# A projection's piece between two links of the inversion: one row of blocks instead of two

## The reference

```python
proj = einsum('bsd,dc->bsc', rmsnorm(x, ln_mix_pre), w_in)
qkv = silu(conv5(proj[q, k, v]))            # depthwise, 5 taps
qa, ka = l2norm(q) * 128**-0.5, l2norm(k)
o_a = delta(qa, ka, va, g_f, beta_f) + flip(delta(flip(qa), flip(ka), flip(va), ...))
o_a = rmsnorm(o_a, norm_a) * silu(z)
# delta, for each chunk: solve (A + I) [u, w] = [v*beta, k*beta*exp(gc)],
# A strictly lower triangular, then a scan over the chunks:
#   v_new = u - w @ state;  o = (q*exp(g)) @ state + a_qk @ v_new
#   state = state * exp(g_last) + (k*exp(g_last - g)).T @ v_new
```

## Time and profile before

| | us |
|---|---|
| median of three executions | 3401.22 |
| lowest, highest | 3398.41, 3410.64 |
| the profiled execution | 3407.34 |
| its span, first to last instruction | 3405.5 |
| TensorE busy in the span | 3172.8 |
| VectorE, ScalarE, GpSimd busy | 1510.9, 1055.3, 366.0 |
| mean granted clock of TensorE | 0.964 |

### The profile page before, as it was taken

One profiled execution on the slowest core, in us unless ns is written; L12 is line 12 of the kernel. 1 busy time (PEld: TensorE's weight loads), 2 busy tenths in 40 slices (PEclk: granted clock), 3 DMA queues, 4 the chain that ended last, 5 costly groups with the idle time before them and its releaser, 6 DMA issues.

```text
span 3405.5 us, 38831 instructions
## 1 busy us (share of the span) xinstructions
PE 3172.8 (93%) x16207; PEld 2581.3 (76%) x16207; DVE 1510.9 (44%) x2112; ACT 1055.3 (31%) x2290; POOL 366.0 (11%) x433
## 2 busy tenths in 40 slices
PE   7999999988899998989989999999999999998997
PEld 4788878877787877877844688888888876777876
DVE  4465555666653122121113344444444567532452
ACT  3444343444433222222310133112112234213452
POOL 0122232232221000000000000000000011001111
PEclk9999999999999998988989999999999999997998
DMA  2211111111011101111261412111111220111010
GB/s 103 63 52 48 37 48 49 34 29 33 29 41 59 59 35 47 38 40 42 91 233 43 170 52 70 50 50 50 50 50 50 93 90 25 62 38 44 26 38 25
DMA packets 59313, 194.86 MB, mean 57 GB/s; under 512 B 7649, under 2 KB 15329, under 8 KB 49410
## 3 DMA queue, kind: packets, MB, share of 16 engines
q1 hardware_dynamic: 58272, 191.29, 16.4%
q10 hardware_dynamic: 866, 1.09, 0.1%
HBM read 158.37 MB, written 33.98 MB: 56 GB/s over the span
## 4 chain that ended last, share of the span: by engine, by line
PE 80%; DVE 9%; ACT 7%; issue 2%; DMA 1%; POOL 1%; SPq 0%; ACTq 0%; POOLq 0%; DVEq 0%
PE ps L2288 18%; PE ps L2290 17%; PE ps L2289 17%; PE ps L1987 5%; PE ps L2165 3%; PE ps L706 3%; PE ps L700 3%; PE ps L1663 2%; DVE ar L1096 2%; PE ps L3166 2%; PE ps L712 1%; PE ps L1628 1%; PE ps L743 1%; PE ps L737 1%; PE ps L3123 1%
## 5 line engine op out<-in xcount | busy, mean ns | idle before, releaser
L2288 PE MATMUL ps<-r,r 128*128 128x512 f32 (+2 forms) x2656 | 1056.8, 398 | 34.3 <-DVE r L228 6.1
L2290 PE MATMUL ps<-r,r 128*128 128x512 f32 (+2 forms) x2656 | 1006.1, 379 | 0.0
L2289 PE MATMUL ps<-r,r 128*128 128x512 f32 (+2 forms) x2656 | 1005.1, 378 | 0.0
L2288 PEld LDWEIGHTS ps<-r,r 128*128 128x128 f32 x2656 | 515.8, 194 | 128.9 <-issue 19.1
L2290 PEld LDWEIGHTS ps<-r,r 128*128 128x128 f32 x2656 | 512.8, 193 | 95.5
L2289 PEld LDWEIGHTS ps<-r,r 128*128 128x128 f32 x2656 | 515.6, 194 | 82.0 <-issue 5.1
L2288 PE MATMUL ps<-r 128*128 128x512 f32 x512 | 199.7, 390 | 0.8 <-DVE r L2281 0.8
L2290 PE MATMUL ps<-r 128*128 128x512 f32 x512 | 199.2, 389 | 0.0
L2289 PE MATMUL ps<-r 128*128 128x512 f32 x512 | 199.2, 389 | 0.0
L2538 DVE TENSOR_TENSOR ar<-ar,ps 128x512 f32<-128x512 f32 x224 | 150.9, 685 | 92.2 <-PE ps L2290 92.1
L1987 PE MATMUL ps<-ar 128*128 128x512 f32 x384 | 170.9, 604 | 8.6 <-DMA ar<-sc_o 6.6
(11 more groups left out here) (319 smaller groups left out, 4287.9 us busy)
## 6 DMA issues: line engine op xcount, KB each, us to landing
ar<-wst SPq DMA_DIRECT2D x76, 1024.0 KB, 4.9
ar<-wst SPq DMA_DIRECT2D x52, 512.0 KB, 3.6
ar<-x SPq DMA_DIRECT2D x16, 512.0 KB, 9.3
ar<-sc_g SPq DMA_DIRECT2D x32, 256.0 KB, 4.7
sc_h<-ar SPq DMA_DIRECT2D x32, 256.0 KB, 2.1
sc_x<-ar SPq DMA_DIRECT2D x16, 512.0 KB, 2.7
ar<-sc_x SPq DMA_DIRECT2D x16, 512.0 KB, 4.3
sc_b<-ar SPq DMA_DIRECT2D x24, 260.0 KB, 2.0
```

The costliest lines, as they stand in the source:

```text
L2288: t.do.matmul(o, l[0], r[0], start=first, stop=False)
L2289: t.do.matmul(o, l[0], r[1], start=False, stop=False)
L2290: return t.do.matmul(o, l[1], r[0], start=False, stop=last)
```

## The change

A piece of a projection becomes one row (three products) with a yield behind it, so the prep and fill threads have twice the slots in every order. The other engines keep their steps: `halved` puts each into the first of two slots and leaves the second empty. The flips keep their rows (13 and 15), the turned tiles of x in the opening order follow the rows 0, 2, 4 and 6. The counts and shapes of the instructions are the same.

```diff
-        plan = [merged((("prep", 0), 2 * NPREP, 0.0, 1.0), (("gates",), 14, 0.15, 0.75), (("bias",), 13, 0.3, 1.0))]
+        plan = [merged((("prep", 0), 4 * NPREP, 0.0, 1.0), (("gates",), 14, 0.15, 0.75), (("bias",), 13, 0.3, 1.0))]
...
-                threads.append((("prep%d" % part, h + 1), NPREP + 8 * (h + 1 in GATES), 0.0, 1.0))
+                threads.append((("prep%d" % part, h + 1), 2 * NPREP + 16 * (h + 1 in GATES), 0.0, 1.0))
...
-                threads.append((("fill", 8 + part), 16, 0.0, 1.0))
+                threads.append((("fill", 8 + part), 32, 0.0, 1.0))
...
-                    if kt % 2 == 1:
-                        yield
+                    yield
...
-                if h == 0 and n < 4:
-                    pe_turn_x(t, 4 + n)
+                if h == 0 and n < 8 and n % 2 == 0:
+                    pe_turn_x(t, 4 + n // 2)
...
-                if n in (6, 7):
-                    pe_flip(t, h, "fq", n - 6, chq[h % 2])
+                if n in (13, 15):
+                    pe_flip(t, h, "fq", (n - 13) // 2, chq[h % 2])
...
+        def halved(steps):
+            for _ in steps:
+                yield
+                yield
...
-                    return both(act_prep0(a, 0), act_prep1(a, 0))
+                    return halved(both(act_prep0(a, 0), act_prep1(a, 0)))
```

More of the change, by code:

```diff
@@ L661, in pe_prep1 @@
                 for n, _ in enumerate(pe_proj(t, h, s)):
-                    if n in (6, 7):
-                        pe_flip(t, h, f, n - 6, src)
+                    if n in (13, 15):
+                        pe_flip(t, h, f, (n - 13) // 2, src)
                     yield
@@ L1036, in make @@
                 if what == "prep":
-                    return both(act_prep0(a, 0), act_prep1(a, 0))
-                return {"gates": act_gates, "prep0": act_prep0, "prep1": act_prep1, "inv": act_inv, "scan": act_scan, "fin": act_fin, "bias": act_bias, "qk": act_qk, "fill": act_fill, "split": act_first_split}[what](a, *of)
+                    return halved(both(act_prep0(a, 0), act_prep1(a, 0)))
+                return {"gates": act_gates, "prep0": lambda a, h: halved(act_prep0(a, h)), "prep1": lambda a, h: halved(act_prep1(a, h)), "inv": act_inv, "scan": act_scan, "fin": act_fin, "bias": act_bias, "qk": act_qk, "fill": lambda a, h: halved(act_fill(a, h)), "split": act_first_split}[what](a, *of)
             for order in plan:
@@ L1248, in make @@
                 if what == "prep":
-                    return both(dve_prep0(v, 0), dve_prep1(v, 0))
+                    return halved(both(dve_prep0(v, 0), dve_prep1(v, 0)))
                 if what == "bias":
                     return idle(1)
-                return {"qk": dve_qk0, "fill": dve_fill, "gates": dve_gates, "prep0": dve_prep0, "prep1": dve_prep1, "inv": dve_inv, "scan": dve_scan, "fin": dve_fin, "split": dve_first_split}[what](v, *of)
+                return {"qk": dve_qk0, "fill": lambda v, h: halved(dve_fill(v, h)), "gates": dve_gates, "prep0": lambda v, h: halved(dve_prep0(v, h)), "prep1": lambda v, h: halved(dve_prep1(v, h)), "inv": dve_inv, "scan": dve_scan, "fin": dve_fin, "split": dve_first_split}[what](v, *of)
             for order in plan:
@@ L1325, in make @@
                 if what == "prep":
-                    return both(idle(NPREP), pool_prep1(p, 0))
-                return idle(1) if what in ("gates", "prep0", "bias", "qk", "fill", "split") else {"prep1": pool_prep1, "inv": pool_inv, "scan": pool_scan, "fin": pool_fin}[what](p, *of)
+                    return halved(both(idle(NPREP), pool_prep1(p, 0)))
+                return idle(1) if what in ("gates", "prep0", "bias", "qk", "fill", "split") else {"prep1": lambda p, h: halved(pool_prep1(p, h)), "inv": pool_inv, "scan": pool_scan, "fin": pool_fin}[what](p, *of)
             for order in plan:
@@ L1404, in make @@
                 if what == "prep":
-                    return both(sp_prep0(sp, 0), sp_prep1(sp, 0))
-                return idle(1) if what in ("scan", "split") else {"gates": sp_gates, "prep0": sp_prep0, "prep1": sp_prep1, "inv": sp_inv, "fin": sp_fin, "bias": sp_bias, "qk": sp_qk, "fill": sp_fill}[what](sp, *of)
+                    return halved(both(sp_prep0(sp, 0), sp_prep1(sp, 0)))
+                return idle(1) if what in ("scan", "split") else {"gates": sp_gates, "prep0": lambda sp, h: halved(sp_prep0(sp, h)), "prep1": lambda sp, h: halved(sp_prep1(sp, h)), "inv": sp_inv, "fin": sp_fin, "bias": sp_bias, "qk": sp_qk, "fill": lambda sp, h: halved(sp_fill(sp, h))}[what](sp, *of)
             for order in plan:
```

## The result

The changed kernel takes 3482.9 us (3480.5 to 3488.9) against 3401.4: the ratio is 1.023, with a 95% interval of 1.021 to 1.025. I had forecast 3443 with 3405 to 3464. It is slower, as forecast, but by 81.5 us where the sum said 42. The profiled execution took 3485.0 (span 3483.1), 2.1 above the median, and its span is 77.6 us longer than the one of before.

The account below looks back on a forecast made before the run. TensorE was taken to bound the kernel, 875.8 us busy of a 957 us stage. Losses of 64.3 less gains of 22.0 gave 42 us slower, from 3401 to a median of 3443, range 3405 to 3464.

Parts of the forecast that it names:

- What bounds it: Recurrent heads stage, 957 us: TensorE bounds it, busy 875.8 us, so a reordering can win or lose only its idle time.
- the mechanism: Engines work queues in order, so a link's copy waits behind a step that waits for a later row; losses 64.3 us.
- Term (a): All eight gate parts: squares or scaled copies stand ahead of Y6's copy on ScalarE; 1.2 us each, 9.6 in all.
- (b): Eight gate parts: an eviction stands ahead of Y5's copy, making it 0.65 us late; 5.2 in all.
- (c): Eight gate parts: an eviction of the gates stands ahead of T1's copy, 0.65 us late; 5.2 in all.
- (d): Ends of odd parts: state update queued behind z's gating product, next part's first state product 4.2 us late; 9.8 in all.
- (e): Parts 1 to 7: convolution step (odd parts also small norm products) ahead of X4's masked copy on VectorE; 8.6 us.
- (f): Plain parts (8 to 15): evictions, flipped keys' copy and squares, and convolution steps ahead of links' copies; 23.8 us in all.
- Rival 3: Ends of odd parts: each 4.2 us stall may bring a clock fall, 12 to 17 us more, 3458; chance 0.17.
- Rival 2: Inside parts: losses are absorbed by shorter waits at the starts of parts; 15 us slower, 3416; chance 0.14.
- Rival 1: Whole stage: evenly spread cover wins and evictions find their row done; 24 us gained, 3377; chance 0.09.
- The gains: TensorE's waits at links, the first Y and the opening, covered by the finer order: 19.3, 2.0 and 0.7, 22.0 us.

Follow-up runs that it names:

- run with GpSimd behind: Changed kernel, but in the four odd parts with a gate GpSimd's two additions start only behind VectorE's last small product of the norms; 3471.2 us, ratio 1.019.
- all steps late: Changed kernel's one-row pieces, but the steps of ScalarE, VectorE, GpSimd and SyncE put by `later` into the second of their two slots; 3382.7 us, ratio 0.9928.

## Why the prediction was wrong in size

The forecast's terms, summed by part, against the differences of the two traces (start of one part to the start of the next):

| parts | forecast | measured |
|---|---|---|
| 0, 2, 4, 6 | +13.0 | +14.2 |
| 8, 10, 12, 14 | +3.5 | +4.6 |
| 1, 3, 5, 7 | +22.3 | +38.1 |
| 9, 11, 13 | +5.0 | +22.4 |
| opening, part 15 and all behind | -1.4 | -1.7 |

- **What bounds it and the mechanism** were right. Each engine worked its queue in order and a link's copy stood behind a step that waited for a later row. The same instructions with the other engines' steps one slot apart differ by 100 us.
- **Term (a)**, 1.2 us: T6 leaves 1.1 to 1.4 us late in all eight parts; taken back alone it is 11.5 us for 9.6.
- **(b), (c)**: from start to start T5 and X1 leave 0.65 to 0.7 us late in parts 0, 2, 4 and 6, as forecast. In the odd ones T5 is 0.4 to 0.7 late, and X1 only 0.3 in parts 3 and 7. The even parts, which have hardly other terms, come out within 1.2 us of the forecast over four parts. They were not taken back singly.
- **(d)**, the size of the wait: 4.2 late was forecast, the rows show 4.1 seven times, and the w waits behind it went at all seven, the ones of L743 at four. Only the clock behind it was left out of the sum.
- **(e)** was mis-sized. It was priced at 1.4 in odd parts with a gate and Y5 was 2.9 to 3.1 us late (in parts 2, 4 and 6 it was 0.5 for the 1.0 forecast). I had taken the small products at what they take alone, though the trace of before already holds four of 1.25 us beside GpSimd's addition:

```profile
474.05 1.25 DVE L1143 TENSOR_TENSOR ar<-ar 128x8 f32<-128x8 f32 x1
```

  The run with GpSimd behind shows their 2 us, and 11.7 us of the time in all; without them the longest wait of Y is 1.1. The Trainium skill, "SBUF — State Buffer" (Who interferes with whom), states this very rule: a VectorE instruction with both inputs in SBUF contends with a GpSimd instruction that reads SBUF, and the one that comes second waits until the other is done. The trace agrees (1.23 and 1.12 us against 0.15). The sum left it out, since the change touches no instruction of either engine. But in the kernel before these products stood behind X4's masked copy (471.32 in the earlier trace rows, the product at 474.05), where Y5 did not wait for them, and the change put them ahead of it.
- **(f)** missed two places in parts 9, 11 and 13: from start to start Y2 waits 1.28 us where it waited 0.19, and Y5 1.16 where it waited 0.58. That is 5 us. So my list of slots was incomplete, and it also lacked the row that is gone ahead of the first Y in these parts (above, 3.1 us). T2, forecast 2.6 late, was:

```profile
752.39 0.60 PE L641 MATMUL ps<-ar 128*128 128x128 f32 x4
...
754.83 0.58 ACT L989 ACTIVATE ar<-ps 128x512 f32<-128x512 f32 x1
755.46 1.40 PE L705 MATMUL ps<-ar 128*128 128x128 f32 x8 [2.47 <-ACT ar L989]
```

- **Rival 3, the clock**, was no alternative to the sum but a part of it, and that is the step that failed: the sum put the clock at nothing, and TensorE is busy 29.7 of the 79.3 us longer with the same products. Its question was whether a 4.2 us stall brings a fall each time. It does, at all seven ends. Its price of 12 to 17 us fits what these falls cost in all (13 to 15), but it was meant as an increase, and three of the seven ends had a fall before the change too, which the page's digits in the earlier trace rows do not show. In half-speed time the increase at the ends is 30.7 of the 44.4 us. The Trainium skill, "TensorE: Matmul & The Clock Gate" (HAM oscillation), has idle stretches throttle the array's clock; the trace agrees, with 0.50 behind each of them. What it left out is the falls behind the other stalls that the change made, behind Y5 of the parts with a gate (503.7, above) and behind the late links of the plain ones. A stall that the sum already holds should have been given its fall in the same line.
- **Rival 2** (absorbed) fell: the starts of parts wait 15.7 and 15.3 us against 15.9 and 14.1. **Rival 1** is the kernel with all steps late: its 24 us of gain exist (25.7), at another placing of the steps.
- **The gains**, 22.0, were sound: 25.7 with all steps late. The opening gained 3.6 for 0.7; with `later` it gained 1.6, so part of it is the placing, and why stays open.

Put together for parts 0 to 14, 43.8 us were forecast and 79.3 measured. Waiting grew by 49.6, near the forecast's 43.8, and partly by luck: Y5 of four parts (6.5 more than priced), the two places of (f) (5) and the first Y (3.1) are 15 us, so other terms were some 9 us too high, of which I know X1, T5 and the even Y5 in part. The other 29.7 are busy time with the same products, and nearly all of it is the lower clock. TensorE has 54.6 us more at half speed there (85.3 against 30.7), 30.7 behind the stalls at the seven ends and 24 behind others, such as those of Y5 (503.7, above) and the late links of plain parts. If it is busy in them, half of each is lost, an estimate of at most 15 and 12 us, 27 of the 29.7. Only the seven ends were tested by a run; the 12 are read from the traces.

## What to carry to other kernels

When a hand-merged order is made finer on one engine, put the other engines' waiting steps behind the last piece that they wait for, not into the first of the new slots: here the same halving is worth 26 us or costs 81, by that alone. A stall that you add to TensorE costs its length, and where the clock falls behind it, the products there at half speed as well; sum both in one line. When an instruction changes its place, look at what the neighbouring engine runs at its new time, even if nothing about the instruction changes.

## What the runs showed of the hardware

- A VectorE product of 128x8 with both inputs in SBUF lasts 1.1 to 1.25 us beside a GpSimd addition of 128x512 and 0.15 us without, and a 128x1024 step 1.99 for 1.3. The long ones started while the addition was under way and ended with it (501.43 and 501.41): a short instruction can hold up a chain for as long as GpSimd's lasts.
- Behind each of the seven stalls of 4.1 us the granted clock was 0.50, and behind the one shown it stayed at 1.00 when 3.81 of the 4.25 us were filled with products that nobody reads, issued ahead of the wait. Seven such fills brought 13 to 15 us. Issued behind the wait, the same products made the kernel 26 us slower.
- In the kernel before, stalls of 2.25 to 2.6 us at the same seven places were followed by a clock of 0.5 at three and not at the other four.
